# Mixer tiles change sides, and group 0's preparation is issued inside the last two in-projection pairs

## The chip, the cores and the metric

The kernel runs on one core of a Trainium2 chip. The metric is the device time of one execution in microseconds (us). Five engines work side by side, each on its own list of instructions, and meet through semaphores: TensorE (PE, matmuls), VectorE (DVE), ScalarE (ACT), GpSimd (POOL) and SyncE (SP), which here issues all DMA transfers. On-chip data lie in SBUF (24 KB regions and larger at fixed byte offsets) and in PSUM, eight banks of 128 x 512 float32.

## The reference

One trunk layer over x (1, 2048, 1024) in float32, with 256 memory tokens:

```
z  = rmsnorm(x) @ w_in                  # (2048, 2816): 22 column tiles of 128
y1 = rwkv7_group(z[:, :1792])           # token shift, low-rank gates, 8 heads x 64, delta-rule scan
y2 = sgu_group(z[:, 1792:])             # gelu, layernorm, 128-frame causal spatial mixing
x += concat(y1, y2) @ w_out
x += mem_cross_attn(rmsnorm(x), mem)    # 4 heads
x += swiglu(rmsnorm(x))                 # width 2816
out = rmsnorm(x)
```

In `rwkv7_group` each token needs a decay w (from tanh and a low-rank product), a rate a, a normalised key kk, and the state update S = S (diag(w) - kk (a kk)^T) + v k^T, y = S r.

## The kernel before, in words

**Stages.** The sequence is cut into two halves of 1024 tokens. A first stage (about 0 to 600 us) projects each half: 11 pairs of jobs ("in", i) for a half, with 8 pairs of memory-token projections ("mem") woven into the first half and 8 pairs that fold the attention weights ("keys", "values") into the second. `ORDER` lists all 38 pairs; `Q_TAIL` is 38. A job of PE is 8 x 6 matmuls of 128 x 512 (three products of high and low float32r parts), its result leaves PSUM by DVE (`z_tile`, `plain_tile`, `fold_out`), gelu tiles pass ACT, and SP stores each 128 x 1024 tile of z to DRAM (`store_z`) as `zT`. The last six jobs of the stage are values 3 (two short ones) and in 9, in 10. Each job's weights come by SP into `w_raw`, ACT writes `w_hi` (`hi`), POOL `w_lo` (`split_job`).

**Mixer.** The second stage (about 600 to 1180 us) takes 16 groups of 128 tokens. `body(k)` on every engine does the recurrent part of group k, the score and solve part of group k+1 and the preparation of group k+2, in one hand-written order. `body(-2, 0, ...)` is thus the preparation of group 0 alone, and `body(-1, 1, ...)` the scores of group 0 with the preparation of group 1. Preparation of group n is: on PE `loras`, `key_norms`, `turn_gate`, `key_scales`, `mix_gate`; on ACT `loras_in`, `lora_tanh`, `roots`, `exps`; on DVE `sum_decays`, `gate_stats`, `reciprocals`, `keys_normed`, `queries`, `mixed`, `decayed`; on POOL `keys`, `gate_norm`, `scaled`. It reads the group's z through `load_keys`, `load_gate`, `load_values`: 10, 1 and 5 DMAs on SP. Groups 0 to 7 lie in the first half's tokens.

**Tail.** From about 1180 us each half passes the output projection, attention and the feed-forward part. Two operand areas are used in turn, a (`a_hi`, `a_lo`) and b (`b_hi`, `b_lo`), 64 KB each.

**What sets the order at the seam.** PE's in-projections read area a until the last job. Before, the mixer's inputs and first tiles (`zin`, `suv`, `wd`, `ad`, `gd`, `kk`, `wx`) stand in the first 32 KB of area a, its outputs for the first half (`y_in_raw`) in the second 32 KB, and the other mixer tiles (`qr`, `atrb`, `qkrm`, `tu`, `bt`, `kt`, ...) in area b; `th` to `v_ln` stand over the weight buffers and `xm`, `n8`, `h_st` over the statistics buffers. So after the last job SP waits for both last stores of z and for all evacuations, then issues the loads of groups 0 and 1; DVE waits for the same stores, clears five tiles (L1802) and then begins `body(-2)`; POOL clears its six and does so too.

In-projection jobs take three PSUM slots in turn (`early`), slot 0, 1 and 3, that is banks 0 to 3 and 6 to 7; a job waits until the job three before it has left.

Of the kernel before, what the change touches and what calls it, by code (L numbers as in the profile page):

```python
# [31 lines left out]
C = 64  # L32
# [24 lines left out]
FIRST_KEYS = ORDER.index(("keys", 0))  # L57
Q_TAIL = len(ORDER)
# [11 lines left out]
def hybrid_block_kernel(nc, xT, memT, gains, weights, shift_mu, w_lora, a_lora, g_lora, head_cols,  # L70
                        kk_rows, lnx_rows, kk_cols, rk_spread, w_spatialT, b_spatial, sgu_ln, consts, cen,
                        head_mean, scan_reset, block_masks, tri_masks, half_ident, tri_wide, outT):
    with ExitStack() as ctx:
# [60 lines left out]
        y_in_raw = place("y_in_raw", [P, KT, TB], F32, OA + 32 * KB)  # L134
        y_in_raw1 = place("y_in_raw1", [P, KT, TB], F32, OB + 32 * KB)
        normed = place("normed", [P, KT, TB], F32, OA)
# [62 lines left out]
        area(OA, OA + 32 * KB)  # L199
# [10 lines left out]
        area(OB, OW)  # L210
# [25 lines left out]
        h_st = rw("h_st", [P, 2, HP, RN])  # L236
        for n, end in used.items():
            assert end <= nc.sbuf_usable_end, (n, end)


        for n in ("const_in in_first in0 in1 in2 in3 xr_in0 xr_in1 sqa_done ws_zero const_ready mixers_done w_raw0 w_raw1 w_hi_done w_lo_done job_done job_out act_in sq_done sumsq_done "
                  "stat_ps stat_rt root_ready m_hi m_lo m_sq m_sum m_stat m_root m_rstd rstd_done z_ext_done z_dif_done z_out_done z_st0 z_st1 carry_done zero_done "
                  "kv_done kvf_hi kvf_lo fold_st0 fold_st1 half_done x_new act_hi act_lo gate_s gate_a prod "
# [14 lines left out]
        def early(pair, u):  # L258

            return slot((0, 1, 3)[(2 * pair + u) % 3])  # L260
# [57 lines left out]
        def _(sp):  # L318
# [58 lines left out]
            for pair, (kind, i) in enumerate(ORDER):  # L377
                for u in range(2):
                    if pair + 2 < Q_TAIL:
                        load_job(pair + 2, u, rows[pair + 2])  # L380
                    if kind == "in":
                        store_z(int(pair >= Q_IN1), i, u)
                    elif kind != "mem":
                        store_fold(pair, kind, i, u)
                if pair == 2:
                    sp.wait_ge(S["act_lo"], KT)
                    sp.wait_ge(S["sumsq_done"], KT)
                    for j in range(4):
                        load_x(1, j)
                if pair == FIRST_KEYS:  # L390
                    load_consts()
            for u in range(2):
                sp.wait_ge(S[f"z_st{u}"], 16 * (1 + HALVES * PAIRS_IN))
            sp.wait_ge(S["job_out"], 2 * Q_TAIL)

# [12 lines left out]
            def load_keys(n):  # L408
                if n >= 2:
                    sp.wait_ge(S["lwa_ps"], n - 1)  # L410
                    sp.wait_ge(S["kk_done"], n - 1)
                    sp.wait_ge(S["rr_done"], n - 1)
# [20 lines left out]

            def store_s(n):
                sp.wait_ge(S["sg_out"], n + 1)
                sp.dma_start(yT_m[HP:2 * HP, :, slice(n * L, (n + 1) * L)].rearrange("m p t -> p m t"), s_out[:]).then_inc(S["sg_st"], 16)
# [88 lines left out]
        def _(pool):  # L525
# [67 lines left out]
            for pair in range(Q_IN1, Q_TAIL):  # L593
# [6 lines left out]
            pool.wait_ge(S["job_out"], 2 * Q_TAIL)  # L600
            for u in range(2):
                pool.wait_ge(S[f"z_st{u}"], 16 * (1 + HALVES * PAIRS_IN))
# [35 lines left out]
            def keys(n, par):  # L638

                r_in, k_in = zin[par][:, 0:4, :], zin[par][:, 4:8, :]  # L640
# [4 lines left out]
                pool.tensor_tensor(k_new[:], k_in, k_mix[:], ALU.mult).then_inc(S["knew_done"], 1)  # L645
# [3 lines left out]
                pool.tensor_tensor(rk[par][:], r_in, k_new[:], ALU.mult).then_inc(S["rk_done"], 1)  # L649

            def scaled(n, par):
                r_in = zin[par][:, 0:4, :]
# [3 lines left out]
                pool.tensor_tensor(aw[:], sig[:, 1, :].rearrange("p (m t) -> p m t", t=L), w_neg[:], ALU.mult).then_inc(S["aw_done"], 1)  # L656
# [3 lines left out]
                pool.tensor_tensor(kt[:], k_new[:], w_neg[:], ALU.mult).then_inc(S["kt_done"], 1)  # L660
# [3 lines left out]
                pool.tensor_tensor(qr[par][:, 1].rearrange("p m a t -> p (m a) t"), r_in.rearrange("p m (a t) -> p (m a) t", a=2),  # L664
                                   wx[:, :, 1:C + 1], ALU.mult).then_inc(S["rr_done"], 1)
                pool.wait_ge(S["kt_done"], n + 1)
                pool.wait_ge(S["rr_done"], n + 1)

            def gate_norm(n):
# [3 lines left out]
                pool.tensor_tensor(v_ln[:], v_hat[:], sln[:, 0, :], ALU.mult).then_inc(S["sg_lw"], 1)  # L673
# [3 lines left out]
                pool.tensor_tensor(v_lnb[:], v_ln[:], sln[:, 1, :], ALU.add).then_inc(S["sg_lb"], 1)  # L677
# [8 lines left out]
            def body(k, par, out=True, scores=True, ahead=True):  # L686
# [4 lines left out]
                if ahead:  # L691
                    keys(k + 2, par)
                    gate_norm(k + 2)
                    scaled(k + 2, par)
# [3 lines left out]
            body(-2, 0, out=False, scores=False)  # L698
# [53 lines left out]
        def _(act):  # L752
# [81 lines left out]
            for pair in range(Q_IN1 + 1, Q_TAIL):  # L834
                kind, i = ORDER[pair - 1]
                for u in range(2):
                    hi(pair, u)
                    if kind == "in" and i >= SHIFT_TILES // 2:
                        gelu(1, i, u)
            for u in range(2):  # L840
                gelu(1, PAIRS_IN - 1, u)


            def evac_x(n, lv):
                b = LEVELS[lv]
                if lv == 0:
                    act.wait_ge(S["x_ps"], 10 * n + 2)
# [9 lines left out]
            def loras_in(n, par):  # L857
# [4 lines left out]
                act.activation(k_sq[:], zin[par][:, 4:8, :], ACT.Square).then_inc(S["ksq_done"], 1)  # L862
# [11 lines left out]
            def lora_tanh(n):  # L874
# [3 lines left out]
                act.activation(th[:], ps[:, 4:6, :], ACT.Tanh, scale=0.5).then_inc(S["th_done"], 1)  # L878
# [13 lines left out]
            def exps(n, par):  # L892
# [4 lines left out]
                act.activation(w_neg[:], cum[:], ACT.Exp, scale=DECAY).then_inc(S["wneg_done"], 1)  # L897
# [3 lines left out]
                act.activation(wx[:, :, 1:C + 1], cum[:].rearrange("p m (a t) -> p (m a) t", a=2), ACT.Exp, scale=-DECAY  # L901
# [3 lines left out]
                act.activation(w_end[par][:], cum[:].rearrange("p m (a t) -> p (m a) t", a=2)[:, :, C - 1], ACT.Exp, scale=-DECAY  # L905
# [62 lines left out]
            act.wait_ge(S["rconst_done"], N_SET)  # L968
            body(-2, 0, state=False, scores=False)
# [5 lines left out]
            def split_y(hf, tiles):  # L975
                for k in tiles:
                    if hf:
                        act.wait_ge(S[f"in{k // 2}"], 16 * (HALVES + 1))
                    act.activation((b_hi if hf else a_hi)[:, k, :], (y_in_raw1 if hf else y_in_raw)[:, k, :], ACT.Copy
# [21 lines left out]
            for hf in range(HALVES):  # L1001
# [32 lines left out]
                one_hi, two_hi = (b_hi, a_hi) if hf else (a_hi, b_hi)  # L1034
# [81 lines left out]
        def _(pe):  # L1116
# [101 lines left out]
            for pair in range(Q_IN1, Q_TAIL):  # L1218
                kind, i = ORDER[pair]
                if pair == FIRST_KEYS:  # L1220
                    pe.wait_ge(S["kvf_lo"], 2)
                for u in range(2):
                    if kind == "in":
                        early_job(pair, u, a_hi, a_lo, TB, split(KT) if pair == Q_IN1 and u == 0 else None)
                    elif kind == "keys":
                        fold_keys(pair, u)
                    else:
                        fold_values(pair, u)


            pe.wait_ge(S["job_out"], 2 * Q_TAIL)

# [30 lines left out]
            def key_norms(n):  # L1263
# [6 lines left out]
                for m in range(HP):  # L1270
                    mm = pe.matmul(ps[32 * m:32 * (m + 1), 6, 0:L], kkc2[:, m, :], k_sq[:, m, :], start=True, stop=True)
# [81 lines left out]
            def scores(n, par, src, need, bank, done):  # L1353
# [3 lines left out]
                if n:  # L1357
                    pe.wait_ge(S["tu_ev"], 12 * n)
                for m in range(HP):
# [196 lines left out]
            pe.wait_ge(S["rconst_done"], N_SET)  # L1556
            body(-2, 0, state=False, behind=False)
# [17 lines left out]
            for hf in range(HALVES):  # L1575
# [4 lines left out]
                one, two = ((b_hi, b_lo), (a_hi, a_lo)) if hf else ((a_hi, a_lo), (b_hi, b_lo))  # L1580
# [87 lines left out]
        def _(dve):  # L1668
# [109 lines left out]
            for pair in range(Q_IN1, Q_TAIL):  # L1778
                kind, i = ORDER[pair]
                for u in range(2):  # L1780
                    if kind == "keys":
                        fold_out(pair, 16 * i, u)
                    elif kind == "values":
                        fold_out(pair, 16 * PAIRS_OUT + 32 * i, u)
                    elif i < SHIFT_TILES // 2:
                        z_tile(1, pair, i, u, True)
                    else:
                        plain_tile(1, pair, i, u)
                if pair == Q_IN1:
                    for n, (dst, raw, high) in enumerate(((kT_lo, kT0, kT_hi), (vT_lo, vT, vT_hi))):  # L1790
                        dve.wait_ge(S["kvf_hi"], n + 1)
                        dve.tensor_tensor(dst[:], raw[:], high[:].bitcast(F32), ALU.subtract).then_inc(S["kvf_lo"], 1)
                if kind == "in" and i == PAIRS_IN - 4:
                    masks()
                if kind == "in" and i == PAIRS_IN - 3:
                    spatial()

# [436 lines left out]
```

## Time and profile before

| | |
|---|---|
| runs, median (lowest to highest) | 3221.84 us (3215.12 to 3226.49), 3 runs |
| profiled execution | 3221.86 us |
| its span on the core | 3220.1 us |
| PE busy | 3087.5 us (96%) |
| DVE, ACT, POOL busy | 35%, 26%, 37% |
| mean granted clock of PE | 0.975 |

The span is what the profiler's rows cover, the execution's time has 1.8 us around it. A granted clock of 1.00 is 2.4 GHz and 0.50 is 1.2 GHz; values between are stretches with both. Times in the rows count from the span's start. L1125 is the line of the matmuls of a job, L1246 of `loras`, L1271 `key_norms`, L1288 `turn_gate`, L1295 `key_scales`, L1328 `mix_gate`, L1362 `scores`.

### The profile page before, as it was taken

The page shows a single profiled execution, that of the slowest core. Times are in us where ns is not written, and L with a number is a line of the kernel's source. Part 1 is how long each engine was busy: PE and PEld are TensorE (multiplying, and loading weights), DVE is VectorE, ACT ScalarE, POOL GpSimd, SP SyncE. Part 2 cuts the span into 40 slices and gives each one's busy share as a digit, 9 for nine tenths or more (in the row PEclk, how much of TensorE's full clock was granted, in tenths as well). Part 3 has the DMA queues.
Part 4 walks back from the last instruction along what each step waited for, and adds up shares of the span by engine and source line. Part 5 has one row for each costly group of instructions (what it writes and reads, how often), then busy time and mean ns, then how long its engine had stood idle before and what let it go on. Part 6 is the DMA issues. An engine that isn't in the chain of part 4 may idle for free.

```text
span 3220.1 us, 63236 instructions
## 1 busy us (share of the span) xinstructions
PE 3087.5 (96%) x27362; PEld 2635.2 (82%) x27362; DVE 1131.6 (35%) x1362; ACT 826.9 (26%) x1382; POOL 1196.5 (37%) x844
## 2 busy tenths in 40 slices
PE   8999999698899889999999999999999999999997
PEld 7888888588888878988888888887998888888885
DVE  6423543266566552323211221244233221221123
ACT  3124112144343341322311111122232321121121
POOL 4655443234344336254222222256426222222224
PEclk9999999789899899999999999999999999999998
DMA  4433544211212221111111111134111111111112
GB/s 159 157 118 105 173 157 152 84 41 49 53 48 63 56 84 63 41 52 46 47 51 46 52 46 47 51 105 150 40 53 46 46 52 46 50 48 46 53 46 78
DMA packets 149017, 233.32 MB, mean 72 GB/s; under 512 B 44353, under 2 KB 101697, under 8 KB 148801
## 3 DMA queue, kind: packets, MB, share of 16 engines
q1 hardware_dynamic: 148800, 230.09, 22.7%
q8 instruction: 178, 2.92, 0.4%
q14 instruction: 39, 0.31, 0.0%
HBM read 186.01 MB, written 44.04 MB: 71 GB/s over the span
## 4 chain that ended last, share of the span: by engine, by line
PE 73%; DVE 3%; issue 2%; POOL 1%; ACT 1%; DVEq 0%; POOLq 0%; ACTq 0%
PE ps L1125 53%; PE ps L1621 6%; PE ps L1246 2%; PE ps L1408 2%; PE ps L1410 2%; PE ps L1392 2%; PE ps L1362 1%; DVE tu L1807 1%; PE ps L1489 1%; DVE normed L2131 1%; POOL w_lo L536 1%; PE ps L1350 1%; PE ps L1318 1%; PE ps L1295 1%; PE ps L1339 1%
## 5 line engine op out<-in xcount | busy, mean ns | idle before, releaser
L536 POOL TENSOR_TENSOR w_lo<-w_raw,w_hi 128x512 fp32r<-128x512 f32 x472 | 654.0, 1409 | 1431.2 <-ACT w_hi L759 1429.6
L1125 PE MATMUL ps<-a_hi,w_hi 128*128 128x512 f32 x2016 | 788.6, 391 | 17.0 <-DVE a_lo L1681 10.0
L1125 PE MATMUL ps<-a_lo,w_hi 128*128 128x512 f32 x2016 | 785.9, 390 | 0.0
L759 ACT ACTIVATE w_hi<-w_raw 128x512 fp32r<-128x512 f32 x472 | 271.9, 624 | 1636.1 <-PE ps L1125 1544.3
L1125 PE MATMUL ps<-a_hi,w_lo 128*128 128x512 f32 x2016 | 621.8, 390 | 0.0
L1125 PE MATMUL ps<-b_hi,w_hi 128*128 128x512 f32 x1312 | 512.1, 390 | 2.0 <-DVE x L2026 1.9
L1125 PE MATMUL ps<-b_lo,w_hi 128*128 128x512 f32 x1312 | 511.0, 389 | 0.0
L1125 PEld LDWEIGHTS ps<-a_hi,w_hi 128*128 128x128 f32 x2016 | 379.4, 188 | 98.6 <-DVE a_lo L1681 10.0
L1125 PEld LDWEIGHTS ps<-a_hi,w_lo 128*128 128x128 f32 x2016 | 379.3, 188 | 79.2
L1125 PEld LDWEIGHTS ps<-a_lo,w_hi 128*128 128x128 f32 x2016 | 379.5, 188 | 78.5 <-issue 0.5
L1125 PE MATMUL ps<-b_hi,w_lo 128*128 128x512 f32 x1312 | 404.8, 390 | 0.0
L2026 DVE TENSOR_TENSOR x<-ps,x 128x1024 f32 (+1 forms) x80 | 97.9, 1224 | 552.8 <-PE ps L1125 546.7
L1125 PEld LDWEIGHTS ps<-b_hi,w_hi 128*128 128x128 f32 x1312 | 246.7, 188 | 54.4 <-issue 2.8
L1125 PEld LDWEIGHTS ps<-b_lo,w_hi 128*128 128x128 f32 x1312 | 246.6, 188 | 51.5 <-issue 0.5
L1125 PEld LDWEIGHTS ps<-b_hi,w_lo 128*128 128x128 f32 x1312 | 246.7, 188 | 51.4
L2098 DVE TENSOR_TENSOR sq<-ps,rstd 128x1024 f32<-128x1024 f32 x44 | 53.9, 1225 | 408.9 <-PE ps L1125 408.9
L1689 DVE TENSOR_TENSOR z_ext<-ps,rstd 128x1024 f32<-128x1024 f32 x44 | 53.9, 1225 | 319.7 <-PE ps L1125 319.2
L1807 DVE COPY_PREDICATED tu<-low,ps 128x256 f32<-128x256 uint8 x192 | 92.8, 508 | 150.7 <-PE ps L1410 128.7
L1410 PE MATMUL ps<-tu,xm 64*64 64x32 f32 x2560 | 133.4, 229 | 0.3 <-issue 0.3
L645 POOL TENSOR_TENSOR k_new<-zin,k_mix 128x512 f32<-128x512 f32 x16 | 20.3, 1270 | 294.8 <-DVE k_mix L1870 294.8
L1410 PEld LDWEIGHTS ps<-tu,xm 64*64 64x64 f32 x2560 | 117.6, 145 | 3.1 <-issue 3.0
L2094 DVE TENSOR_TENSOR work<-ps,rstd 128x1024 f32<-128x1024 f32 x44 | 53.9, 1225 | 180.9 <-PE ps L1125 180.2
(251 smaller groups left out, 3915.0 us busy)
## 6 DMA issues: line engine op xcount, KB each, us to landing
w_raw<-in_weights SPq DMA_DIRECT2D x228, 512.0 KB, 3.5
zT<-z_out SPq DMA_DIRECT2D x44, 512.0 KB, 3.8
w_raw<-kvw SPq DMA_DIRECT2D x32, 512.0 KB, 3.2
suv<-zT SPq DMA_DIRECT2D x16, 512.0 KB, 4.7
x<-in_xT SPq DMA_DIRECT2D x16, 512.0 KB, 5.7
outT<-normed SPq DMA_DIRECT2D x16, 512.0 KB, 4.0
in_raw<-in_xT SPq DMA_DIRECT2D x7, 1024.0 KB, 11.2
zin<-zT SPq DMA_DIRECT2D x48, 128.0 KB, 2.3
```

The lines of the kernel that those rows point to most:

```text
L536: pool.tensor_tensor(low_t[:, u, part, :], w_raw[:, u, part, :], high[:, u, part, :].bitcast(F32), ALU.subtract).then_inc(S["w_lo_done"], 1)
L759: act.activation(split_into(pair)[0][:, u, part, :], w_raw[:, u, part, :], ACT.Copy).then_inc(S["w_hi_done"], 1)
L1125: mm = pe.matmul(to[:, nb, 0:w], wt[:, u, k, :], r[:, k, nb * w:(nb + 1) * w], start=(k == 0 and r is hi_in and wt is w_hi), stop=(k == kn ...
L1246: mm = pe.matmul(cols(bank, m), lhs[:, m * P:(m + 1) * P], rhs[:, (m // 2) * C:(m // 2) * C + L], start=True, stop=True)
L1392: mm = pe.matmul(unit(h, 2 * g * (lv > 0) + e, 2 * L + g * C * (lv == 0) + mh * 32, 32), atrb[par][lane(a), e, 2 * mh + g, 0, :], t_u, sta ...
L1408: pe.matmul(unit(a, *t_at, 32), u_u, x_u.rearrange("p (n two b) -> p n two b", two=2, b=b)[:, :, 0, :], start=True, stop=True)
L1410: mm = pe.matmul(unit(h, 2 * g + 1, (e + 1) * C + mh * 32, 32), x_u, u_u.rearrange("p (n two b) -> p n two b", two=2, b=b)[:, :, 1, :], st ...
L1621: mm = pe.matmul(to, st[:, k, at:at + P], wt[:, 0:2, k, :], start=(k == 0 and n == 0 and t % 2 == 0), stop=(k == KT - 1 and n == 2), skip_ ...
L1689: dve.tensor_tensor(z_ext[:, u, 1:TB + 1], flat(src), rstd[:], ALU.mult).then_inc(S["job_out"], 1)
L1807: dve.copy_predicated(out, mask, data).then_inc(S[done], 1)
L2026: dve.tensor_tensor(at_k(x, k), flat(slot(u)).unsqueeze(1), at_k(x, k), ALU.add).then_inc(S["job_out"], 1)
L2094: dve.tensor_tensor(work[:, 0, :], flat(slot(0)), rstd[:], ALU.mult).then_inc(S["job_out"], 1)
```

## The change

`zin` ... `bn` move to the first 32 KB of area b, `y_in_raw` and `normed` to area b as well, the other mixer tiles to area a, and the tail's halves use the areas in exchanged order. For group 0 alone ten tiles (`th`, `sig`, `cum`, `k_mix`, `k_sq`, `k_new`, `v_hat`, `v_ln`, `w_neg`, `aw`) get homes of their own that the in-projection does not use; `at(name, n)` picks them. With `FIRST_AHEAD` = 36 (the pair in 9):

- SP issues the 32 loads of groups 0 and 1 ahead of pair 36's stores, after job 71 (values 3) is done; those of group 2 come after the last stores, as before.
- The last four jobs use PSUM slots 0 and 1 only, each waiting for the evacuation of the job two before it.
- `body(-2)` disappears; its calls stand between the jobs of pairs 36 and 37 on each engine. Only `queries`, `decayed` (DVE), `scaled_query`, `scaled_key`, `key_query` (POOL) wait for the last job, since they write area a.
- Of the five tiles that DVE cleared, it clears two (`atrb[0]`, `qkrm[0]`) behind its last evacuation; POOL clears the other three.

```diff
+FIRST_AHEAD = len(ORDER) - 2
-            return slot((0, 1, 3)[(2 * pair + u) % 3])
+            return slot(u if pair >= FIRST_AHEAD else (0, 1, 3)[(2 * pair + u) % 3])
...
# SP
             for pair, (kind, i) in enumerate(ORDER):
+                if pair == FIRST_AHEAD:
+                    for u in range(2):
+                        sp.wait_ge(S[f"z_st{u}"], 16 * (1 + PAIRS_IN))
+                    sp.wait_ge(S["job_done"], 2 * FIRST_AHEAD)
+                    for n in range(2):
+                        load_keys(n)
+                        load_gate(n)
+                        load_values(n)
...
-            for n in range(2):
-                load_keys(n)
-                load_gate(n)
-            for n in range(2):
-                load_values(n)
             load_keys(2)
             load_gate(2)
...
# POOL
-            pool.wait_ge(S["job_out"], 2 * Q_TAIL)
-            for u in range(2):
-                pool.wait_ge(S[f"z_st{u}"], 16 * (1 + HALVES * PAIRS_IN))
+            pool.wait_ge(S["job_done"], 2 * FIRST_AHEAD)
+            pool.wait_ge(S["w_lo_done"], 4 * (FIRST_AHEAD + 1))
...
-            body(-2, 0, out=False, scores=False)
+            split_job(FIRST_AHEAD + 1, 0)
+            key_mixed(0, 0)
+            gate_norm(0)
+            rates(0)
+            split_job(FIRST_AHEAD + 1, 1)
+            pool.wait_ge(S["job_done"], 2 * Q_TAIL)
+            scaled_query(0, 0)
+            scaled_key(0)
+            for t in (xm, atrb[1], qkrm[1]):
+                pool.memset(t[:], 0.0).then_inc(S["late_zero"], 1)
+            key_query(0, 0)
+            pool.wait_ge(S["wend_done"], 1)
+            for u in range(2):
+                pool.wait_ge(S[f"z_st{u}"], 16 * (1 + HALVES * PAIRS_IN))
             body(-1, 1, out=False)
...
# ACT
-            act.wait_ge(S["rconst_done"], N_SET)
-            body(-2, 0, state=False, scores=False)
+            for pair in range(Q_IN1 + 1, Q_TAIL):
+                kind, i = ORDER[pair - 1]
+                if pair == FIRST_AHEAD + 1:
+                    act.wait_ge(S["rconst_done"], N_SET)
+                    loras_in(0, 0)
+                for u in range(2):
+                    hi(pair, u)
+                    if kind == "in" and i >= SHIFT_TILES // 2:
+                        gelu(1, i, u)
+                    if pair == FIRST_AHEAD + 1 and u == 0:
+                        lora_tanh(0)
+                        act.wait_ge(S["fold_st0"], FOLDED)
+                        roots(0)
+                        exps(0, 0)
+            for u in range(2):
+                gelu(1, PAIRS_IN - 1, u)
+            act.wait_ge(S["job_done"], 2 * Q_TAIL)
             body(-1, 1, state=False)
...
# PE
-                    pe.wait_ge(S["job_out"], 2 * pair + u - 2)
+                    pe.wait_ge(S["job_out"], 2 * pair + u - 2 + (pair >= FIRST_AHEAD))
...
-            pe.wait_ge(S["rconst_done"], N_SET)
-            body(-2, 0, state=False, behind=False)
+            for pair in range(Q_IN1, Q_TAIL):
...
+                    if pair == FIRST_AHEAD and u == 0:
+                        pe.wait_ge(S["rconst_done"], N_SET)
+                        pe.wait_ge(S["stat_rt"], HALVES)
+                        loras(0, 0)
+                        key_norms(0)
+                        turn_gate(0, 0)
+                    elif pair == FIRST_AHEAD:
+                        key_scales(0)
+                    elif pair > FIRST_AHEAD and u == 0:
+                        mix_gate(0, False)
+            pe.wait_ge(S["job_out"], 2 * Q_TAIL - 1)
             body(-1, 1, state=False)
...
# DVE
-            for t in (atrb[0], atrb[1], qkrm[0], qkrm[1], xm):
-                dve.memset(t[:], 0.0).then_inc(S["const_ready"], 1)
...
-            dve.wait_ge(S["rconst_done"], N_SET)
-            body(-2, 0, state=False, scores=False)
+            for pair in range(Q_IN1, Q_TAIL):
+                kind, i = ORDER[pair]
+                for u in range(2):
+                    if pair > FIRST_AHEAD and u == 1:
+                        dve.wait_ge(S["job_done"], 2 * Q_TAIL)
+                        queries(0, 0)
+                        decayed(0)
...
+                        plain_tile(1, pair, i, u)
+                    if pair == FIRST_AHEAD and u == 0:
+                        dve.wait_ge(S["fold_st0"], FOLDED)
+                        dve.wait_ge(S["fold_st1"], FOLDED)
+                        sum_decays(0)
+                        gate_stats(0)
+                        reciprocals(0)
+                    elif pair == FIRST_AHEAD:
+                        keys_normed(0, False)
+                    elif pair > FIRST_AHEAD and u == 0:
+                        mixed(0)
...
+            for t in (atrb[0], qkrm[0]):
+                dve.memset(t[:], 0.0).then_inc(S["const_ready"], 1)
+            dve.wait_ge(S["const_ready"], 9)
             body(-1, 1, state=False)
```

## Rows read from the trace of the kernel before

**Rows 1.** The page's 40 slices of 80.5 us, PE's busy tenths.

```profile
PE   8999999698899889999999999999999999999997
```

**Rows 2.** Windows: engine busy (instructions) PE, PEld, DVE, ACT, POOL, then granted clock, DMA.

```profile
600.36:631.27 30.91, 7.62 (x54) 6.46 (x53) 14.54 (x22) 9.33 (x15) 11.42 (x14) 0.59 0.42 115
634.65:661.48 26.83, 24.18 (x599) 21.80 (x591) 15.54 (x31) 11.06 (x22) 8.93 (x7) 0.83 0.16 42
```

**Rows 3.** Timeline of DVE: start, duration, line, count, idle before.

```profile
567.83 1.23 DVE L1689 TENSOR_TENSOR z_ext<-ps,rstd 128x1024 f32<-128x1024 f32 x1 [9.75 <-PE ps L1125]
600.47 1.23 DVE L1689 TENSOR_TENSOR z_ext<-ps,rstd 128x1024 f32<-128x1024 f32 x1 [9.65 <-PE ps L1125]
605.76 0.91 DVE L1802 MEMSET atrb<- 128x1024 f32 x1 [4.06 <-DMA zT<-z_out]
623.22 0.71 DVE L1892 TENSOR_SCALAR v_hat<-ps,bn 128x512 f32<-128x512 f32 x1
626.07 1.12 DVE L1919 SCALAR_TENSOR_TENSOR qr<-kk,wx 128x512 f32<-128x512 f32 x1
629.32 0.77 DVE L1927 TENSOR_TENSOR bt<-kk,aw 128x512 f32<-128x512 f32 x1
633.31 1.34 DVE L1807 COPY_PREDICATED atrb<-tri,ps 128x512 f32<-128x512 uint8 x2 [3.22 <-PE ps L1362]
```

**Rows 4.** Timeline of SP's issues, last before pair 36 and first of group 0.

```profile
559.62 1.04 SPq L362 DMA_DIRECT2D kvw<-folded  x2
605.49 0.46 SPq L405 DMA_DIRECT2D wd<-zT  x1
```

**Rows 5.** Timeline of ACT, group 0's first two steps.

```profile
612.69 0.36 ACT L859 ACTIVATE wd<-wd 64x192 f32<-64x192 f32 x1 [9.85 <-DMA zin<-zT]
616.71 1.02 ACT L878 ACTIVATE th<-ps 128x1024 f32<-128x1024 f32 x1 [3.14 <-PE ps L1246]
```

**Rows 6.** Timeline of PE, group 0's preparation and first scores.

```profile
616.60 0.43 PE L1271 MATMUL ps<-k_sq,kkc 128*32 128x128 f32 x8
616.96 0.66 PE L1288 MATMUL ps<-cst,suv 128*128 128x128 f32 x4
624.08 1.23 PE L1295 MATMUL ps<-n,kkr 64*128 64x128 f32 x8 [6.46 <-DVE v_hat L1892]
626.69 1.97 PE L1328 MATMUL ps<-ws,v_lnb 128*64 128x128 f32 x16 [1.39 <-POOL v_lnb L677]
631.27 1.99 PE L1362 MATMUL ps<-qr,bt 64*64 64x128 f32 x32 [2.60 <-POOL qr L664]
```

**Rows 7.** Chain that ended last, pieces in time: start, us, what.

```profile
643.04 3.71 PE ps L1246 x16
657.45 0.65 PE ps L1295 x8
658.69 1.09 PE ps L1246 x8
659.78 1.02 PE ps L1328 x16
```

**Rows 8.** Windows of 2 us, columns as in rows 2; last two are DMA share, GB/s.

```profile
560.00:562.00 2.00, 2.00 (x11) 1.65 (x10) 0.00 (x0) 0.00 (x0) 0.00 (x0) 1.00 1.25 360
```

**Rows 9.** Windows of 1 us, PE alone: busy, granted clock, DMA share, GB/s.

```profile
602.00:603.00 1.00, 0.00 (x0) 0.80 0.00 0
616.00:617.00 1.00, 1.00 (x14) 0.88 0.63 147
```

**Rows 10.** One line's durations over the run, ns: min/median/max.

```profile
L1919 DVE SCALAR_TENSOR_TENSOR qr<-kk,wx x16: 683/824/1820, 626.1 to 1138.0; 128x512 f32<-128x512 f32 x16
```

**Rows 11.** Timeline of DVE, the decay sum of groups 1, 14 and 15.

```profile
649.52 1.23 DVE L1865 TENSOR_TENSOR_SCAN cum<-reset,sig 128x512 f32<-128x512 f32 x1
1091.01 1.22 DVE L1865 TENSOR_TENSOR_SCAN cum<-reset,sig 128x512 f32<-128x512 f32 x1
1127.67 1.22 DVE L1865 TENSOR_TENSOR_SCAN cum<-reset,sig 128x512 f32<-128x512 f32 x1
```

More of the change, by code:

```diff
@@ L432, in load_gate @@
                 sp.dma_start(suv[n % 2][:], zT_t[14:22, :, n * L:(n + 1) * L].rearrange("m p t -> p m t")).then_inc(S[f"zs{n % 2}"], 16)
+            for pair, (kind, i) in enumerate(ORDER):
+                if pair == FIRST_AHEAD:
[7 more added lines that the diff above has]
+                for u in range(2):
+                    if pair + 2 < Q_TAIL:
+                        load_job(pair + 2, u, rows[pair + 2])
+                    if kind == "in":
+                        store_z(int(pair >= Q_IN1), i, u)
+                    elif kind != "mem":
+                        store_fold(pair, kind, i, u)
+                if pair == 2:
+                    sp.wait_ge(S["act_lo"], KT)
+                    sp.wait_ge(S["sumsq_done"], KT)
+                    for j in range(4):
+                        load_x(1, j)
+                if pair == FIRST_KEYS:
+                    load_consts()
+            for u in range(2):
+                sp.wait_ge(S[f"z_st{u}"], 16 * (1 + HALVES * PAIRS_IN))
+            sp.wait_ge(S["job_out"], 2 * Q_TAIL)
             def store_s(n):
@@ L592, in _ @@
                     square_tile(in_raw[:, k, :], (k, KT + k), k == 0)
-            for pair in range(Q_IN1, Q_TAIL):
+            for pair in range(Q_IN1, FIRST_AHEAD + 1):
                 split_pair(pair)
@@ L833, in _ @@
                 act.activation(dst[:], raw[:], ACT.Copy).then_inc(S["kvf_hi"], 1)
[L834 to L841, printed above, removed]
             def evac_x(n, lv):
@@ L1217, in _ @@
                         stats(1)
[L1218 to L1231, printed above, removed]
             def cols(bank, i):
@@ L1270, in key_norms @@
                 for m in range(HP):
-                    mm = pe.matmul(ps[32 * m:32 * (m + 1), 6, 0:L], kkc2[:, m, :], k_sq[:, m, :], start=True, stop=True)
+                    mm = pe.matmul(ps[32 * m:32 * (m + 1), 6, 0:L], kkc2[:, m, :], at("k_sq", n)[:, m, :], start=True, stop=True)
                 mm.then_inc(S["kn_ps"], 1)
@@ L1554, in body @@
                     merge(b, q, 4)
-            pe.wait_ge(S["rconst_done"], N_SET)
-            body(-2, 0, state=False, behind=False)
+            for pair in range(Q_IN1, Q_TAIL):
+                kind, i = ORDER[pair]
+                if pair == FIRST_KEYS:
+                    pe.wait_ge(S["kvf_lo"], 2)
+                for u in range(2):
+                    if kind == "in":
+                        early_job(pair, u, a_hi, a_lo, TB, split(KT) if pair == Q_IN1 and u == 0 else None)
+                    elif kind == "keys":
+                        fold_keys(pair, u)
+                    else:
+                        fold_values(pair, u)
+                    if pair == FIRST_AHEAD and u == 0:
[9 more added lines that the diff above has]
+            pe.wait_ge(S["job_out"], 2 * Q_TAIL - 1)
             body(-1, 1, state=False)
@@ L1578, in _ @@
                 lo0 = KT * HALVES + 3 * KT * hf
[L1580 removed]
+                one, two = ((a_hi, a_lo), (b_hi, b_lo)) if hf else ((b_hi, b_lo), (a_hi, a_lo))
                 def phase(first_q, pairs, hi_in, lo_in, kn, stat=None, lo_wait=None, halves=False):
@@ L1776, in spatial @@
                 dve.tensor_scalar(hc[:, 1, :], hc[:, 0, :], -1.0, 1.0, ALU.mult, ALU.add).then_inc(S["const_ready"], 1)
[L1778 to L1796, printed above, removed]
-            for u in range(2):
-                dve.wait_ge(S[f"z_st{u}"], 16 * (1 + HALVES * PAIRS_IN))
-            dve.wait_ge(S["job_out"], 2 * Q_TAIL)
-            for t in (atrb[0], atrb[1], qkrm[0], qkrm[1], xm):
-                dve.memset(t[:], 0.0).then_inc(S["const_ready"], 1)
-            dve.wait_ge(S["const_ready"], 12)
             triangles = tri[:].rearrange("p m w t -> p (m w t)")
```

139 lines of the change are left out of this document (85 added, 54 removed).

## Prediction

> **What bounds the kernel now.** I read the 40 slices first. PE is at nine tenths nearly everywhere; the deepest hole is slice 8, about 563 to 644 us, with 6 tenths [rows 1]. It lies where the in-projection ends and the mixer begins. A window from the end of the last job's matmuls to the first scores shows 30.91 us in which PE is busy for 7.62 us [rows 2]. Outside this hole the change leaves PE the same work in the same order, so the sum is made at this seam, from the end of the last job to a common mark on the other side. The mark is the end of DVE's two copies that take group 0's first scores out of PSUM: 633.31 + 1.34 = 634.65 us [rows 3]. From there `body(-1)` is the same program in both kernels. The last job's result starts to leave at 600.47, 0.11 us behind its last matmul, so the job ends at 600.36 [rows 2, 3]. Old seam: 634.65 - 600.36 = 34.3 us.
>
> The timelines show what fills it. SP's first load comes only at 605.49 [rows 4], held by the last store of z (DVE's clearing starts then too, with the store named as what ended its wait [rows 3]). ACT gets its first input 7.20 us later, at 612.69 [rows 4, 5]. Preparation then takes a chain through all engines until the first scores at 631.27 [rows 6]. So the seam is a chain of latencies, not of any engine's work.
>
> **The new seam, step by step.** The loads no longer need a store of the second half, since groups 0 and 1 lie in the first.
>
> 1. Start of the loads. SP's last issue before pair 36 is the fold stores at 559.62, 1.04 us long; SP is free at 560.66 [rows 4]. The new wait (job 71 done) is over by then. Behind it on SP stand 32 issues, some 17 us at the old pace, and behind those the stores of pair 36. The first of these was ready at about 570 and goes at 578; its buffer is wanted again 20 us later, so this costs nothing. Both weight loads of pair 37 are already out.
>
> 2. PE's new wait. `loras(0)` stands behind job 72, whose end is 567.7 (evacuation 567.83 less 0.11) [rows 3]. With the old 7.20 us, ACT's tanh could start at 560.66 + 7.20 = 567.86, and PE 0.5 us later. But the queues are full at the start: weights and fold stores give a DMA share of 1.25 and 360 GB/s in 560 to 562 [rows 8]. I add 1.0 us, so PE stands still for 567.86 + 1.0 + 0.5 - 567.7 = 1.7 us. Lower end 0.6 (no queueing), upper end 6 (the ten transfers behind all that is queued, as much again as the whole issue time of ten). Behind PE's wait stands everything on PE, so it counts in full. ACT's `hi` for job 74 is behind the same wait, but is needed 12 us later.
>
> 3. PE's own work goes inside the jobs and lengthens them. At full clock: `loras` twice the 1.09 us of eight records, 2.2; `key_scales` 0.65; `mix_gate` 1.02 [rows 7]; `key_norms` 0.43, `turn_gate` 0.66 [rows 6]. Sum 5.0 us. At half clock the same five are 3.71 [rows 7], 0.43, 0.66, 1.23 and 1.97 [rows 6], 8.0 us. I take 5.0, since dense jobs surround them, and 0.1 us for each of the five hand-overs, 0.5.
>
> 4. Other waits of PE inside the pairs: none. From the end of `loras` the chain for `key_scales` runs over ACT and DVE; before, it took from 616.71 (`th`) to 623.22 + 0.71, 7.2 us [rows 3, 5], and with the start delay about 8. PE has `key_norms`, `turn_gate` and job 73 (10.9 us) to fill, together 12 us. Cover left: 4 us; were it gone, PE would wait the excess twice (here and, through POOL's `gate_norm`, at `mix_gate`). The extra change of ACT's function table, since a gelu now follows the exponentials, is inside this cover. Two PSUM slots instead of three want an evacuation of 1.23 us within a job of 10.9, so nothing. The last job so ends 1.7 + 5.0 + 0.5 = 7.2 us later than before, at 607.6.
>
> 5. Behind the last job. DVE: start 0.1, `queries` 1.12, `decayed` 0.77, the last evacuation 1.23, two clearings of 0.91 with 0.15 between, the two copies 1.34 [rows 3], and 0.2 of semaphores: 0.1 + 1.12 + 0.77 + 1.23 + 2.1 + 1.34 + 0.2 = 6.9 us. PE's first scores need `decayed` and POOL's `scaled_query`, ready some 2 us behind the job; 1.99 us at half clock [rows 6] end at 4.1, ahead of the copies at 5.4. The second scores need the last evacuation, and end before their copy as well. POOL's three clearings and ACT's identities fall in the same 6 us. DVE sets this end.
>
> Port sharing. GpSimd now runs `scaled_query` beside DVE's `queries`. The trace has `queries` between 683 and 1820 ns, 824 in the middle [rows 10], so company costs it up to 0.7 us; I stay with group 0's own 1.12. The Trainium skill, "GPSIMD Engine Reference", section 1 Specifications, says that GpSimd's SBUF interface is shared with VectorE and contended when a VectorE instruction has two SBUF inputs, which both have here; by the slowest row the 6.9 would be 7.6.
>
> 6. New seam: 7.2 + 6.9 = 14.1 us against 34.3. Gain 20.2 us.
>
> 7. Clock. From the mark to the next group's start, 26.83 us, the granted clock is 0.83 in the mean [rows 2], and `loras(1)` in it takes 3.71 us where two warm batches of eight take 2.2 [rows 7]. After the change PE comes warm to this stretch, but it stands for two short times behind the last job. I credit 1.0 us, between -1 and 5.
>
> Sum: 20.2 + 1.0 = 21.2 us. The profiled execution took 3221.86 us with a span of 3220.1; its time is that of the median, 3221.84, so no correction is needed. Forecast 3200.7, rounded 3201 us. Best ends together (wait 0.6, credit 5) give 3195.6; bad ends (wait 6, work at half clock 8.0, DVE 7.6, credit -1) give 20.2 - 4.3 - 3.0 - 0.7 - 1 = 11.2 and 3211.
>
> The added `rk_done` wait in `load_keys` is on a product that POOL finishes ahead of one already waited for; the exchange of areas moves no operation in the tail. Both cost nothing.
>
> **Rivals.**
>
> A. The wait at `loras` is long and cools PE. For it: the clock fell 2.2 us after PE stopped at 600.36 (0.80 in 602 to 603, so at 602.6) and came back only at about 616.2, 3 us after work began again [rows 9]. Then `loras` and a part of job 73 run at 1.2 GHz. Price: 4.3 us more wait, 3.0 for the work at half clock, 1.5 for 3 us of job 73, together 8.8: gain 12.4, 3209.5 us. Against it: the expected wait of 1.7 is shorter than those 2.2. The Trainium skill, "TensorE: Matmul & The Clock Gate", part "HAM oscillation — how this bites in real kernels", warns of just this: idle gaps between bursts of matmuls put the engine back to half rate each time. By that rule the 1.7 us are harmless if short enough, which the row bears out so far. Chance 0.15.
>
> B. The preparation is not hidden. ACT and POOL have the weights of job 75 to split between the steps of the preparation, in order; if each step comes 5 us late, PE waits at `key_scales` and again at `mix_gate`, 10 us, and 5 of wait at the loads stay. Gain 21.2 - 15 = 6, 3216 us. Against it are the 4 us of cover and POOL's 33% load. Chance 0.08.
>
> C. Slower than before: the group loop falls into a worse pattern of clock. The decay sums of groups 1 and 15 are 478.15 us apart, 34.15 per group; the last step is 36.66 [rows 11]. Were all 14 steps like the last, the loop would lose 14 x 2.51 = 35 us against a gain of 21.2: 3236 us. From 1.5 us a group on this decides. For it: the clock already changes within each group, and the seam changes when the loop starts. Against it: the one long step stands among shorter ones, so the pattern is not held from group to group. Chance 0.05.
>
> **How the numbers follow.** Forecast 0.72, A 0.15, B 0.08, C 0.05. What a measurement can tell from no change is 0.3%, 9.7 us. The forecast and A lie past it but for a tail of each (together 0.02): faster 0.85. B and those tails: same 0.10. C: slower 0.05. The range: 3195.6 to 3211 for the bounds, and the three runs of before spread over 11.4 us, so a median may be some 4 us off at either end: 3190 to 3213.
>
> **What would show it.** SP's first load at 560 to 562; PE's `loras` (L1246 of before) at 568 to 571; the last evacuation at 610 to 613 behind the two products; the copies' end at 613 to 618; five preparation steps inside the jobs with no wait above 0.5 us but the first; the tail's start about 21 us earlier, with 34 us per group between. Wrong it is if PE waits at `key_scales` or `mix_gate`, if job 73 runs at half clock, or if the group loop takes over 490 us.

## The result, and the profile after

| | before | after |
|---|---|---|
| median of 6 runs each | 3223.55 us (3215.12 to 3226.67) | 3197.61 us (3185.91 to 3204.70) |
| ratio | | 0.992, 95% interval 0.9895 to 0.9944 |
| profiled execution, its span | 3221.86, 3220.1 us | 3185.91, 3184.0 us |

The kernel is faster, by 0.8% or 26 us in these medians, where 21 us were forecast (3201 us). Runs of the changed kernel spread widely: over all measurements below there are 30 with a mean of 3198.3 us (3182.1 to 3225.8), beside 56 of the kernel before with a mean of 3223.1 (3208.0 to 3249.7). The profiled execution after was nearly its fastest run, so its seam can be compared with that of before, its span can't.

The hole in slice 8 [rows 1] is gone; PE's slices of the page after:

```profile
PE   8999999988889899999999999999999999999997
```

The seam on PE, in the timeline of the kernel after (L1285 is `loras`, L1310 `key_norms`, L1327 `turn_gate`, L1334 `key_scales`, L1367 `mix_gate`, L1403 `scores`):

```profile
568.01 1.13 PE L1285 MATMUL ps<-wd,wl 128*128 128x128 f32 x8 [1.31 <-ACT wd L898]
568.97 1.06 PE L1285 MATMUL ps<-ad,al 128*128 128x128 f32 x8
569.96 0.43 PE L1310 MATMUL ps<-k_sq_first,kkc 128*32 128x128 f32 x8
570.56 0.66 PE L1327 MATMUL ps<-cst,suv 128*128 128x128 f32 x4 [0.18 <-DMA suv<-zT]
582.08 0.71 PE L1334 MATMUL ps<-n,kkr 64*128 64x128 f32 x8
593.83 1.09 PE L1367 MATMUL ps<-ws,v_lnb 128*64 128x128 f32 x16
608.44 1.94 PE L1403 MATMUL ps<-qr,bt 64*64 64x128 f32 x32 [2.41 <-DVE bt L1964]
```

In brackets stands the idle time before a group. Inside the jobs PE waits once, 1.31 us for ACT's tanh, and 0.18 for `suv`; at `key_scales` and `mix_gate` it does not wait. The scores follow the last job where the whole of [rows 6] stood between. Behind them, DVE's timeline (evacuations of jobs 72 and 75, then the clearings and the copies that answer to the last of [rows 3]):

```profile
566.81 1.23 DVE L1750 TENSOR_TENSOR z_ext<-ps,rstd 128x1024 f32<-128x1024 f32 x1 [9.75 <-PE ps L1179]
606.06 0.69 DVE L1956 SCALAR_TENSOR_TENSOR qr<-kk,wx 128x512 f32<-128x512 f32 x1 [9.99 <-PE ps L1179]
606.67 1.67 DVE L1964 TENSOR_TENSOR bt<-kk,aw_first 128x512 f32<-128x512 f32 x1
608.26 1.21 DVE L1750 TENSOR_TENSOR z_ext<-ps,rstd 128x1024 f32<-128x1024 f32 x1
609.88 0.91 DVE L2058 MEMSET atrb<- 128x1024 f32 x1 [0.40 <-DVE z_ext L1750]
610.95 0.91 DVE L2058 MEMSET qkrm<- 128x1024 f32 x1 [0.16 <-issue]
611.90 1.33 DVE L1842 COPY_PREDICATED atrb<-tri,ps 128x512 f32<-128x512 uint8 x2
```

The last job's matmuls end at 605.95 (`queries` at 606.06 less 0.11), the mark is 611.90 + 1.33 = 613.23. From job 72's evacuation to the mark it is 46.42 us; before it was 634.65 - 567.83 = 66.82 [rows 3]. The difference, 20.4 us, is what the change took out of the seam, against 20.2 forecast. I call this distance D in what follows; the forecast's "seam" is D less the 32.53 us of jobs 73 to 75 before.

SP's first load and ACT's first step, the two that answer to [rows 4] and [rows 5]:

```profile
559.77 0.60 SPq L407 DMA_DIRECT2D wd<-zT  x1
```

```profile
567.50 0.36 ACT L898 ACTIVATE wd<-wd 64x192 f32<-64x192 f32 x1 [12.89 <-DMA zin<-zT]
```

Job 72 left 1.0 us earlier in this profile than before (566.81 for 567.83), so the times that the prediction names are met 1.0 us early. Allowing for that, the first load (559.77) and the copies' end (613.23) lie in the stretches named; the last evacuation, at 608.26, is still some 0.7 us ahead of its own (610 to 613).

### The profile page after: what moved, and what is told of

Its sections match the earlier page's. It is cut to its first block, busy times and chain, and to the rows that moved or that the text cites. A ratio compares the mean times of both kernels' runs of the same rounds, so it can differ in the third digit from the quotient of the medians.

```text
span 3184.0 us, 63259 instructions
## 1 busy us (share of the span) xinstructions
PE 3064.6 (96%) x27362; PEld 2611.8 (82%) x27362; DVE 1129.6 (35%) x1359; ACT 827.6 (26%) x1383; POOL 1198.4 (38%) x847
## 4 chain that ended last, share of the span: by engine, by line
PE 74%; DVE 4%; issue 2%; POOL 1%; ACT 1%; SPq 0%; DMA 0%; DVEq 0%; POOLq 0%; ACTq 0%
PE ps L1179 54%; PE ps L1682 6%; PE ps L1449 2%; PE ps L1285 2%; PE ps L1451 2%; PE ps L1433 2%; PE ps L1403 1%; DVE tu L1842 1%; POOL w_lo L561 1%; DVE normed L2202 1%; PE ps L1530 1%; PE ps L1334 1%; PE ps L1357 1%; PE ps L1389 1%; PE ps L1367 1%
```

## The experiments

D, what follows it to group 1's decay sum, the loop from there to group 15's decay sum, and the rest of the span behind that, in each profile (the granted clock is that of the loop):

| kernel | D | mark to group 1 | loop | clock | rest |
|---|---|---|---|---|---|
| before | 66.8 | 14.9 | 478.2 | 0.91 | 2092.4 |
| before, e1 | 67.0 | 14.9 | 469.2 | 0.93 | 2094.6 |
| after | 46.4 | 15.0 | 464.9 | 0.96 | 2090.9 |
| after, e2 | 46.3 | 16.3 | 483.0 | 0.89 | 2094.2 |
| after, e8 | 46.3 | 14.8 | 472.4 | 0.92 | 2093.5 |
| after, e11 | 46.5 | 14.9 | 469.1 | 0.93 | 2100.1 |
| e3 | 53.0 | 14.9 | 469.6 | 0.93 | 2097.1 |
| e4 | 54.8 | 15.1 | 473.3 | 0.94 | 2091.9 |
| e5 | 43.4 | 14.5 | 472.0 | 0.93 | 2092.5 |
| e6, e10 | 42.3, 42.3 | 15.1, 15.1 | 476.2, 466.9 | 0.93, 0.94 | 2100.2, 2099.3 |
| e7, e9 | 42.3, 42.3 | 14.6, 14.6 | 478.5, 472.7 | 0.91, 0.92 | 2088.0, 2097.7 |

### e1 and e2: both kernels again

No edit in either.

> The kernel before, unchanged, for a second profile of its group loop. Theory: the 14 steps from the decay sum of group 1 to that of group 15 took 478.2 us before and 464.9 us after the change, and this 13.3 us is chance of the clock in the loop, not the change. It expects a second profile of before to give a loop other than 478 by several us (anywhere from 462 to 485), with a seam (end of the last job to the end of the two copies of group 0's first scores) of 34.3 +- 0.5. Rival: the change itself makes the loop faster. It expects 478 +- 3 again.

> The changed kernel, unchanged. Chance of the clock: seam 13.9 +- 0.5 as in its first profile (7.3 of it behind the last job), but another loop, 462 to 485 us instead of 464.9; median 20 to 27 us below before. Rival, the change speeds the loop: loop 465 +- 3 again.

e1, one run, took 3215.18 us: D 67.0, loop 469.2, nine us shorter than in the first profile of the same kernel. e2: 3191.72 us median of 4 runs, ratio 0.989 (0.9855 to 0.9925), 30.0 us under before where 20 to 27 were expected; D 46.3 as in the first profile after, but a loop of 483.0 against 464.9. So the 13.3 us by which the first two profiles' loops differ need no change to explain them: the same program varies by 18 us there. The two loops of the changed kernel, windows of the first profile and of e2 (busy of PE, PEld, DVE, ACT, POOL, granted clock):

```profile
628.25:1093.13 464.88, 411.95 (x13043) 374.77 (x13035) 297.76 (x587) 197.39 (x419) 202.00 (x168) 0.96 0.21 54
```

```profile
629.82:1112.77 482.95, 441.59 (x13045) 403.52 (x13043) 298.38 (x586) 197.81 (x419) 201.22 (x168) 0.89 0.20 52
```

DVE, ACT and POOL were as busy in both; only PE's matmuls took longer, at a lower clock.

### e3: loads early, preparation not

```diff
 # PE (likewise on ACT, DVE, POOL): body(-2)'s calls go behind the last job
-                    if pair == FIRST_AHEAD and u == 0: loras, key_norms, turn_gate
-                    elif pair == FIRST_AHEAD: key_scales
-                    elif pair > FIRST_AHEAD and u == 0: mix_gate
+            loras(0, 0); key_norms(0); turn_gate(0, 0)
+            key_scales(0); mix_gate(0, False)
             body(-1, 1, state=False)
```

> Of the change only the new places and the early loads: group 0's whole preparation stands behind the last job again (its first tanh excepted, which needs the loads alone). Theory (the seam is a chain of latencies: 5.1 us to the first load, 7.2 for the loads, then the preparation): loras starts 0.2 us behind the last job, th at 2.5, and from th to the mark before took 634.65 - 616.71 = 17.9 us: seam 20.4 us against 34.3 before and 13.9 after, a gain of 13.9, so about 6.5 us slower than the whole change, 3209 or 0.996 of before. Rival (the preparation inside the jobs brings the most, the loads were hidden by it): seam above 26 us, gain under 8 us.

D is 53.0, a seam of 20.5 where 20.4 was expected. In the time it is 0.9939 (0.9919 to 0.9959) of before: 3203.79 against 3221.73 us, 17.9 us less where 13.9 us (3209 us) were expected. DVE's timeline of e3 shows the chain of latencies back in its place:

```profile
603.87 0.69 DVE L1895 TENSOR_SCALAR sig_first<-th_first 128x1024 f32<-128x1024 f32 x1
609.16 0.71 DVE L1926 TENSOR_SCALAR v_hat_first<-ps,bn 128x512 f32<-128x512 f32 x1
615.25 0.78 DVE L1961 TENSOR_TENSOR bt<-kk,aw_first 128x512 f32<-128x512 f32 x1
619.25 1.33 DVE L1839 COPY_PREDICATED atrb<-tri,ps 128x512 f32<-128x512 uint8 x2 [3.22 <-PE ps L1403]
```

So two thirds of the 20.4 us come from the loads, which no longer wait for the last store and their own landing, and one third (6.6 us) from the preparation inside the jobs, which costs PE its own time there. e3 also keeps three of the five clearings off DVE, but that gains nothing at this seam: before, the last of them ended at 610.43, ahead of ACT's first input at 612.69 [rows 5].

### e4: a longer wait at loras

```diff
-                    for n in range(2):
-                        load_keys(n)
-                        load_gate(n)
-                        load_values(n)
+                    load_gate(0)
+                    load_values(0)
+                    load_gate(1)
+                    load_keys(0)
+                    load_values(1)
+                    load_keys(1)
```

> The changed kernel with the ten key loads of group 0 issued behind seven others (gate and values of group 0, gate of group 1), so PE's wait at loras is longer by 7 x 0.5 = 3.5 us, about 4.8 instead of 1.3. Theory of the forecast (a wait under 2.2 us keeps PE at 2.4 GHz, rival A was right on what a longer one does): the clock falls in the wait, loras takes about 3.7 instead of 2.1 us and the first 1 to 3 us of job 73 run at 1.2 GHz: 3.5 + 1.6 + 1 = 6 us slower than the changed kernel in the last job's end. Rival (the clock is not touched by such a wait): 3.5 us alone.

3206.99 us, 0.996 (0.9944 to 0.9976) of before. D is 54.8: 8.4 us more than the changed kernel, not 6. The wait grew by 6.1 us, not 3.5, as this row of PE's timeline shows; SP needed 3.23 us to issue one of the seven loads now in front (why is not shown; in the changed kernel the same stores and weight loads stood before its loads, and the first two took 0.60 and 0.71 us):

```profile
573.64 2.05 PE L1287 MATMUL ps<-wd,wl 128*128 128x128 f32 x8 [7.40 <-ACT wd L900]
```

```profile
559.98 3.23 SPq L407 DMA_DIRECT2D gd<-zT  x1
```

PE alone, before the wait's end, in the preparation and in job 73 (busy, granted clock, DMA):

```profile
565.90:573.64 7.74, 0.34 (x2) 0.69 0.68 175
573.64:578.68 5.04, 5.04 (x28) 0.50 0.31 75
578.68:589.80 11.12, 11.12 (x50) 0.98 0.31 94
```

The clock fell within the wait, the three products took 5.04 us where they took 3.2 before job 73 in the changed kernel, and job 73 lost some 0.2. Together that is 6.1 + 1.8 + 0.2 = 8.1 of the 8.4 us. So rival A's mechanism exists, with 2.0 us for the cold work and not 4.5 (`key_scales` and `mix_gate` came when the clock was back). In the changed kernel, with its wait of 1.31 us, the granted clock was 1.00 in every window of 2 us from 566 to 572. The Trainium skill, "TensorE: Matmul & The Clock Gate", part "HAM oscillation — how this bites in real kernels", has idle gaps put PE back to half rate; by that rule the longer wait costs more than itself, and this run agrees, with 0.50 in its second row.

The 2.2 us that the forecast took from one row of before are no limit, though. Behind the last job PE stood for 2.41 us both in the first profile after and in e2. In the first the scores then took 1.94 us, at half clock (row 608.44 above); in e2 they did not:

```profile
608.69 1.10 PE L1403 MATMUL ps<-qr,bt 64*64 64x128 f32 x32 [2.41 <-DVE bt L1964]
```

### e5 and e6: the steps one job later, a clearing in a gap

```diff
 # e5, PE; ACT, DVE and POOL follow
-                    if pair == FIRST_AHEAD and u == 0:      # loras, key_norms, turn_gate
+                    if pair == FIRST_AHEAD and u == 1:
-                    elif pair == FIRST_AHEAD:               # key_scales
+                    elif pair > FIRST_AHEAD and u == 0:
-                    elif pair > FIRST_AHEAD and u == 0: mix_gate(0, False)
+            mix_gate(0, False)                              # behind the last job
 # e6, DVE, on top of e5
-            for t in (atrb[0], qkrm[0]): dve.memset(...)
+            dve.memset(atrb[0][:], 0.0)
+            def take_first(n, par):
+                if n == 0: dve.memset(qkrm[0][:], 0.0)
```

> The changed kernel with group 0's loras, key norms and turn of the gate behind job 73 instead of 72, key scales behind job 74, mix_gate behind job 75, and DVE's mixed behind the second scores. Theory (the wait of 1.3 + 0.2 us at loras is the loads' landing, and 3 to 4 us of the 12 us cover at key scales are spare): no wait at loras, none at key scales, and mix_gate's 1.1 us falls in PE's 2.4 us gap behind the last job. Last job ends 1.5 + 1.1 = 2.6 us earlier against job 71 than in the changed kernel; what follows it stays 7.3 us to the mark. Rival (the steps are so tight that one of them waits elsewhere): a wait of over 1 us at key scales or before the first scores, and less than 1.5 us gained.

> As e5, and DVE clears qkrm[0] only in its wait for PE's first pairs. Theory (DVE's own chain sets the 7.3 us behind the last job): the mark comes 1.07 us earlier behind it, 6.2 us; with e5's 2.6 together 3.7 us off the seam, 10.2 instead of 13.9. Rival (PE's scores set it): the mark stays at 7 us or more. In the time of the whole 3.7 us are 0.1% of the kernel, below what the rounds tell; the profile decides.

e5 (one run, 3191.18 us): D 43.4, 3.0 us less than the changed kernel, with no wait at `loras` or `key_scales` in PE's waits. e6: 3202.28 us, 0.9914 (0.9884 to 0.9944); D 42.3, another 1.1 less. DVE's timeline of e6 has the second clearing where DVE waited for PE's first pairs:

```profile
608.24 1.34 DVE L1839 COPY_PREDICATED atrb<-tri,ps 128x512 f32<-128x512 uint8 x2
609.72 0.91 DVE L1855 MEMSET qkrm<- 128x1024 f32 x1
610.92 1.29 DVE L1839 COPY_PREDICATED tu<-low,ps 128x256 f32<-128x256 uint8 x2 [0.28 <-DVE qkrm L1855]
```

Both theories hold: the 1.5 us of wait was only the loads' landing, and DVE's chain, not PE, sets the time from the last job to the mark. But e6 moves its clearing behind the mark, so not all of its 1.1 us is a gain: from job 72's evacuation to group 1's decay sum it is 57.9 us in e5 and 57.4 in e6.

### e7: PE kept busy in the gaps

```diff
+            def fill(times):
+                for _ in range(times):
+                    pe.matmul(ps[:, 5, :], cent[:], bsp[:].rearrange("p m t -> p (m t)"), start=True, stop=True)
...
             mix_gate(0, False)
+            fill(1)
...
+                    if b == 0: fill(1)     # behind the second scores, and behind first_pairs
```

> As e6, with three matmuls of 128 x 512 float32 (1.1 us each, result unused) in PE's gaps behind the last job, behind the first scores and behind the first pairs. Theory (the clock falls in these gaps, and loras(1), 3.7 us at 1.2 GHz against 2.1, pays for it; a warm PE then also enters the group loop): clock 1.00 from the last job to loras(1), and from the mark to the decay sum of group 1 12.5 to 13.5 us instead of 15.0; 2 us faster than e6. Rival (latencies between the engines set this stretch, not the clock): 14.5 or more, no gain.

3191.10 us, 0.9885 (0.9853 to 0.9917): 11 us under e6 in the median where 2 were expected, but not for the reason given. From the mark to group 1's decay sum it is 14.6 us, 0.5 less than e6 and not 1.5 to 2.5, and `loras(1)` still ran at half clock. PE in e7 (busy, granted clock, DMA):

```profile
612.00:614.00 2.00, 1.22 (x34) 1.00 0.10 25
614.00:616.00 2.00, 1.64 (x65) 1.00 0.29 75
616.00:618.00 2.00, 1.96 (x35) 0.51 0.33 77
626.00:636.00 10.00, 10.00 (x178) 0.50 0.01 2
```

The same windows in e6:

```profile
614.00:616.00 2.00, 2.00 (x54) 0.50 0.39 106
616.00:618.00 2.00, 1.60 (x49) 0.50 0.60 149
626.00:636.00 10.00, 9.74 (x239) 1.00 0.01 3
```

The fill held the clock at 1.00 until 616 where e6 had 0.50 already. It did not close all gaps, as the first two rows show, so the run neither shows nor excludes that gaps start a fall. What it does show is that continuous work did not end one: the clock stayed at 0.50 past 636 with PE busy all the time, where e6 was back at 1.00. e2, without any fill, has such a stretch too (21.60 of 22.00 us busy in 618 to 640, at 0.50).

The decay sum lies too early to see what this costs. The 26.83 us of step 7 [rows 2] run from the mark to the first matmul of group 1's recurrent part (`v_tok`, `qkrm`). The same stretch in e6 and in e7 (all engines, then granted clock and DMA):

```profile
609.58:636.66 27.08, 24.31 (x591) 21.96 (x591) 17.00 (x32) 11.48 (x24) 11.00 (x9) 0.81 0.19 54
610.28:643.51 33.23, 32.00 (x593) 27.84 (x593) 16.79 (x32) 11.51 (x24) 11.80 (x10) 0.64 0.16 45
```

With the fill it is 6 us longer, and again in the second pair (27.05 in e10, 33.28 in e9). Of the eleven profiles without fill ten have 26.5 to 27.1 us and one, e2, 35.0; so the fill goes with the long stretch, but is not needed for it.

### e8 to e11: the four kernels compared

e8 and e11 are the changed kernel, e9 is e7's, e10 is e6's.

> The changed kernel again, a third profile of it. Chance of the clock: its loop (group 1's to group 15's decay sum) was 464.9 and 482.9 us with granted clock 0.96 and 0.89; a third lies anywhere from 460 to 485, on the same line of loop against clock (about 2.6 us for 0.01). Rival (two kinds of the kernel differ by the change): no such line, loops of the changed kernel apart from those of before at the same clock. With ten more runs its median should be 20 to 24 us under that of before if the seam's 20.4 us is all; 27 or more speaks for a part of the gain in the loop.

> e7's kernel again. Its first runs lay 11 us under e6's in the median (3191.1 against 3202.3, six and seven runs), though its profile showed no gain behind the mark. Theory (that was chance of the clock in the loop): median within 5 us of e10's in this call, about 3198. Rival (the fill pays, later than the mark): again 8 us or more under e10's.

> e6's kernel again. Seam 53.3 us from job 71's evacuation to the mark, as in e6. Theory: 4 us under the changed kernel's median of this call, since 4.0 us of seam are gone, and 24 to 29 under before.

> The changed kernel, a fourth profile: seam 57.3 us as in the three before; loop somewhere between 462 and 485 us, at a granted clock that goes with it (0.96 at 465, 0.92 at 472, 0.89 at 483). Median 20 to 28 us under before.

e8: 3202.90 us, 0.9933 (0.9902 to 0.9964), 22.1 us under before, with a loop of 472.4 us at 0.92: as the theory had it. The ratios to before of the other three were 0.9901 (0.9874 to 0.9929) for e9 at 3186.50 us, 0.9931 (0.9905 to 0.9957) for e10 at 3194.32, and 0.9923 (0.9899 to 0.9947) for e11 at 3195.36. e11 came as expected, 25 us under before. e10's D of 42.3 repeats e6's exactly, yet its median lies 1 us under the changed kernel's where 4 were expected. e9 lies 8 us under e10 where at most 5 were expected.

Together e7 and e9 have a mean of 3190.0 us in 12 runs (standard error 1.6), e6 and e10 3198.3 in 13 (1.7). A difference of 8.3 us with a standard error of 2.3 is hardly chance. That the fill is its cause is not shown, since the profiles don't have it: all that follows the mark sums to 2581.0 and 2585.0 us in e7 and e9, and to 2591.5 and 2581.3 in e6 and e10. The loops with fill are no shorter, and the stretch up to group 1 is 6 us longer. Behind the loop both profiles with fill had the better clock in the first 100 us, with 0.98 and 0.88 against 0.83 and 0.85; but the four profiles of the changed kernel had 0.88 to 0.97 there. PE in e6 and in e7:

```profile
1100.86:1200.86 100.00, 93.17 (x1599) 0.83 0.27 86
1103.35:1203.35 100.00, 90.07 (x1640) 0.98 0.29 91
```

With 3190.0 it is the fastest version tried, 1.0% under before and 8 us under the changed kernel (30 runs, 3198.3, standard error 1.9).

## Why the prediction was right

The mechanism was right: the seam was a chain of latencies that hung on the loads' start, and taking it apart gave 20.4 us at the seam where 20.2 were forecast. That the two agree within 0.2 us is in part luck, since three terms were off by 0.2 to 0.4 us each and cancelled. The 1.0 us credited to the clock did not come, and some 4 to 5 us of the measured gain, about twice their standard error, have no place in the sum.

**Sum.** Term by term, forecast and measured in the first profile after:

| step | forecast | measured |
|---|---|---|
| SP's first load to ACT's tanh (2) | 8.2 | 7.73 |
| PE's wait for the loads (1, 2) | 1.7 | 1.31 + 0.18 |
| five products at full clock and hand-overs (3) | 5.5 | 5.1 |
| waits at `key_scales`, `mix_gate` (4) | 0 | 0 |
| behind the last job to the mark (5) | 6.9 | 7.28 |
| seam | 14.1 | 13.9 |
| clock from the mark on (7) | 1.0 gained | 0.1 lost |

The third row is what is left of the three jobs' lengthening: 605.95 - 566.70 is 39.25 us from job 72's end to the last job's, 32.64 before (600.47 - 567.83 [rows 3]), so 6.61 more, less 1.49 of waits.

**The cover (4).** `v_hat` ended at 577.46 and `key_scales` ran at 582.08, 4.6 us of spare time against 4 forecast. Rival B had no ground; e5 moved all steps a job later and still met no wait.

**DVE's chain (5).** It was mis-sized by 0.4 us. `decayed` took 1.67 us against 0.77, while `queries` took 0.69 against 1.12; together 2.36 for 1.89. GpSimd's products beside them, two after and one before (`qr<-zin,wx` is `scaled_query`, `kt` is `scaled_key`):

```profile
606.11 1.68 POOL L694 TENSOR_TENSOR qr<-zin,wx 128x512 f32<-128x512 f32 x1 [20.61 <-PE ps L1179]
607.75 1.73 POOL L688 TENSOR_TENSOR kt<-k_new_first,w_neg_first 128x512 f32<-128x512 f32 x1
629.50 1.62 POOL L664 TENSOR_TENSOR qr<-zin,wx 128x512 f32<-128x512 f32 x1
```

GpSimd was thus busy beside `decayed` in both kernels; what changed is who came first. After, `decayed` began at 606.67 behind GpSimd's 606.11 and ended 0.55 us behind its end. Before, it began at 629.32 [rows 3], ahead of GpSimd's 629.50, and took 0.77. The Trainium skill, "GPSIMD Engine Reference", section 1 Specifications, has the two engines contend when a VectorE instruction has two SBUF inputs. The trace agrees for `decayed` after; `queries`, which began 0.05 us ahead of GpSimd, paid nothing. The prediction's upper end by the slowest row was 7.6 us, and 7.28 were measured.

**The clock (7).** This step failed. It had PE come warm to the stretch behind the mark. PE was at full clock when the last job ended, but the clock fell at the end of the 2.41 us behind it, so the scores took 1.94 us where they had taken 1.99 before. The stretch that the step priced, from the mark to group 1's recurrent part (661.48 before, 640.20 after), was as long and as cold as before:

```profile
613.23:640.20 26.97, 24.23 (x591) 21.89 (x591) 15.55 (x31) 11.06 (x22) 10.19 (x8) 0.81 0.17 46
```

That is 26.97 us at 0.81 for 26.83 at 0.83 [rows 2]. In e8 and e11 it is 26.8; in e2 it is 35.0, so the bounds of -1 to 5 us were too narrow as well. A warm PE would not have helped either: in e2, e6, e7, e9 and e10 the clock was still 1.00 at the mark, and the stretch took 27.1 us in e6 and e10 and 33 to 35 in the others. What sets the clock behind the mark stays open.

**Rival C.** The loop does vary as C said, by 18 us for one and the same kernel, but it did so in both kernels alike: 464.9 to 483.0 in four profiles of after, 469.2 and 478.2 in two of before. It widens the runs' spread and gives no sign to the change.

**Open.** Medians and means gained more than D did: 24.8 us in the means of 56 and 30 runs (standard error 2.1) against 20.4, and e3 18.9 against 13.8; but e6 with e10 24.8 against 24.5. The profiles show no such part outside the seam: what follows the mark sums to 2582.1 us in the mean of the two of before and to 2582.3 in that of the four of after. Single ones lie between 2570.8 and 2593.5, too far apart to exclude 5 us.

## What to carry to other kernels

At a seam between two stages read the first transfer's wait: here it hung on a buffer place, not on data, and moving tiles to a region that is free early gave two thirds of the gain. Count a moved step's own time on the engine that bounds: of the 13.2 us that moving the preparation took off the end (20.5 us behind the last job in e3, 7.3 in the changed kernel), 5.1 came back inside the jobs and 1.5 as a new wait. Where the runs of one kernel differ by 20 us, judge an edit of 5 us by the distance between two fixed events in the profile, and read a later event too: e6 moved work behind the mark, and the 6 us that go with e7's fill stand behind the decay sum.

## What the runs showed of the hardware

PE's clock stayed at 1.2 GHz in stretches in which its rows show it busy all the time: 10.00 of 10 us in 626 to 636 of e7. The work there was small float32 matmuls (64 x 32 and 128 x 128). The same gap of 2.41 us before the same matmuls was followed by half clock in one execution of a kernel and by full clock in another. One program's loop of 14 groups had a mean granted clock between 0.89 and 0.96 from execution to execution, and 18 us went with it.

Where VectorE and GpSimd products of 128 x 512 float32 overlapped at the seam, the one that began second was the long one: `decayed` 1.67 us behind GpSimd and 0.77 ahead of it, GpSimd's `scaled_query` 1.68 behind VectorE, where GpSimd products with no such neighbour took 1.26 to 1.30.

A single DMA issue took SP 3.23 us in e4 where the next took 0.43, with some 2 MB of weights and stores issued just before; the cause is not shown.
